# A two-layer decoder step on one core: the first expert pair's rows by a one-hot matmul, four projections ahead of the router, the window-cache copy last

## The reference, cut to what matters

```python
def moe(h, router_w, router_bias, w_gate, w_up, w_down):
    score = sigmoid(h @ router_w)                     # 16 experts
    ... # top-2 experts inside the best of 4 groups; gate = normalised scores
    for e in range(16):
        hid = silu(h @ w_gate[e]) * (h @ w_up[e])     # 1024 -> 512
        out = out + gate[..., e:e + 1] * (hid @ w_down[e])
    return out

def layer_tail(x, mix, p_i, ...):
    h = layer_norm(ALPHA * x + mix, ln1_g, ln1_b)
    h = layer_norm(ALPHA * h + moe(h, ...), ln2_g, ln2_b)
    return h + sigmoid(h @ ple_gate) * (p_i @ ple_proj)
```

## Time and profile before

| | us |
|---|---|
| median of 3 runs | 1172.66 |
| the three runs | 1172.66, 1162.14, 1172.76 |
| the profiled execution | 1171.1 |
| its span, first to last instruction | 1169.3 |
| PE busy in it | 1051.3 (90%) |
| DVE busy | 469.3 (40%) |
| ACT busy | 297.0 (25%) |
| DMA, mean over the span | 297 GB/s |

### The profile page before, as it was taken

How to read it: one execution, slowest core, us unless ns; L and a number is a source line. 1 busy time by engine, 2 the same in 40 slices (tenths; PEclk the granted TensorE clock), 3 DMA queues, 4 the chain that set the end, 5 groups by cost and what they waited for, 6 DMA issues and landing times. The chain is left out here.

```text
span 1169.3 us, 14744 instructions
## 1 busy us (share of the span) xinstructions
PE 1051.3 (90%) x5243; PEld 658.4 (56%) x5243; DVE 469.3 (40%) x1383; ACT 297.0 (25%) x765; POOL 133.3 (11%) x121
## 2 busy tenths in 40 slices
PE   7899998698799999899799989779989999989868
PEld 5688775587554444344477875345755344444347
DVE  2769898932331112011355977472161111111132
ACT  2211798700321111111220015362051011101031
POOL 0000013300001000000004724452000000000000
PEclk9899998799988999999999998889988999999989
DMA  8744696675959999999556975949368899999901
GB/s 287 248 163 149 220 278 215 198 281 198 399 225 408 427 429 428 425 427 428 213 216 235 339 262 178 370 136 382 128 265 370 363 427 426 428 428 426 417 4 38
DMA packets 88943, 347.36 MB, mean 297 GB/s; under 512 B 14690, under 2 KB 52578, under 8 KB 72322
## 3 DMA queue, kind: packets, MB, share of 16 engines
q1 hardware_dynamic: 81186, 313.57, 69.3%
q10 hardware_dynamic: 5376, 24.40, 5.3%
q0 software_dynamic: 2304, 8.39, 1.8%
HBM read 331.66 MB, written 23.04 MB: 303 GB/s over the span
## 5 line engine op out<-in xcount | busy, mean ns | idle before, releaser
L1097 PE MATMUL mh<-expert_ring,x_packed 128*64 128x512 f32 x768 | 173.0, 606 | 14.6 <-DMA expert_ring<-in_moe_w_up 12.7
L1349 DVE TENSOR_TENSOR hid<-mh,silu_gate 128x512 f32<-128x512 f32 x16 | 11.1, 692 | 374.8 <-PE mh L1097 325.9
L1097 PEld LDWEIGHTS mh<-expert_ring,x_packed 128*64 128x64 f32 x768 | 58.2, 140 | 126.3 <-issue 124.3
L1119 PE MATMUL mo<-expert_ring,hid_T 128*64 128x512 f32 x384 | 89.1, 618 | 1.4 <-ACT hid_T L1218 1.4
L495 PE MATMUL ss<-xT,expert_ring 128*128 128x264 f32 x384 | 90.0, 395 | 0.0
L1563 PE MATMUL na<-xT,expert_ring 128*128 128x264 f32 (+1 forms) x336 | 78.8, 398 | 6.1 <-DMA expert_ring<-in_nsa_w_in 3.3
L495 PEld LDWEIGHTS ss<-xT,expert_ring 128*128 128x128 f32 x384 | 73.8, 195 | 13.8 <-issue 0.8
L1563 PEld LDWEIGHTS na<-xT,expert_ring 128*128 128x128 f32 (+1 forms) x336 | 64.6, 193 | 20.2 <-DMA expert_ring<-in_nsa_w_in 4.1
L506 PE MATMUL ss<-xT,expert_ring 128*128 128x264 f32 x256 | 64.1, 406 | 6.1 <-ACT z L385 6.1
L1179 PE MATMUL mg<-acc,expert_ring 128*128 128x264 f32 x256 | 61.7, 406 | 7.2 <-ACT acc L883 7.2
L1097 PE MATMUL mh<-expert_ring_more,x_packed 128*64 128x512 f32 x256 | 58.3, 609 | 7.7 <-DMA expert_ring_more<-in_moe_w_up 3.6
(11 more groups left out here) (377 smaller groups left out, 1541.1 us busy)
## 6 DMA issues: line engine op xcount, KB each, us to landing
expert_ring<-in_moe_w_down SPq DMA_DIRECT2D x24, 2048.0 KB, 22.3
expert_ring<-in_moe_w_gate SPq DMA_DIRECT2D x24, 2048.0 KB, 17.2
expert_ring<-in_moe_w_up SPq DMA_DIRECT2D x24, 2048.0 KB, 23.5
expert_ring<-in_ssd_w_in SPq DMA_DIRECT2D x10, 2048.0 KB, 7.9
expert_ring_more<-in_moe_w_gate SPq DMA_DIRECT2D x8, 2048.0 KB, 14.7
expert_ring_more<-in_moe_w_up SPq DMA_DIRECT2D x8, 2048.0 KB, 19.2
expert_ring_more<-in_moe_w_down SPq DMA_DIRECT2D x8, 2048.0 KB, 22.5
expert_ring<-in_cmp_pages SPq DMA_DIRECT2D x40, 256.0 KB, 4.5
```

The source lines that it names most:

```text
L1097: last = mm(hb[w][s * CAP:(s + 1) * CAP, :], xg[:, k, s * CAP:(s + 1) * CAP], unit(6 * i + 2 * w + s)[:, k * FF:(k + 1) * FF], start=k == ...
L1119: last = mm(ob[2 + a][s * CAP:(s + 1) * CAP, :], ht[:, k, s * CAP:(s + 1) * CAP], unit(6 * i + 4 + s)[:, o:o + 512], start=k == 0, stop=k ...
L1349: V.tensor_tensor(hid[:], hb[1][:], sg[:], ALU.mult).then_inc(hid_ok, 1)
```

## The change

Five edits, four of them in the tail:

1. **Projections 0 to 3** move to right behind PE's part of `ln_a`, into four separate banks. ACT copies their results between the root (L880) and the gain-and-bias steps (L883) of `ln_a`. Projections 4 and 5 stand where 0 and 1 stood, 6 and 7 right behind the rank matmuls.
2. **Pair 0's rows** come from a matmul of `xtok` with `sel1`: 2 x 4 x 3 matmuls of 128 columns. The indirect DMA of pair 0, its `turn_rows` and the slot tokens of pair 0 ahead of it go.
3. **Slot tokens** of all eight pairs are computed inside `gate_up(0)`, one pair's three matmuls ahead of each step k of the up half. `other_slots()` goes; of it the turn of `gover` stays as `gates_over()`.
4. **Unit 7** is loaded right after `wple`, ahead of the wait for the projections. Unit 6 waits as before.
5. **The cache copy** goes from ACT's queue in the Mamba block to SP's queue, behind the last weight load of layer 1.

```diff
@@ Mamba block @@
                     sp.wait_ge(conv_out, 32)
-                    sp.wait_ge(win_out, 16)
...
-                    act.dma_start(O["win_old"], I["cache_win"][:, 1:, :]).then_inc(win_out, 16)
@@ Norm @@
-            def act(self, act):
+            def act(self, act, between=None):
...
                 nc.scalar.activation(self.rs[:, 1, :], self.pv[:, 0:T], ACT.Sqrt, scale=1.0 / D, bias=epst[:, 0:1]).then_inc(s_sqrt, 1)
+                if between is not None:
+                    between()
                 for k in range(KD):
@@ tail, SP @@
+                        load_unit(sp, L, 7, unit(7))
                         sp.wait_ge(e_proj, KD * (L + 1))
-                        for n in range(6, 8):
-                            load_unit(sp, L, n, unit(n))
+                        load_unit(sp, L, 6, unit(6))
...
+                        if L == 1:
+                            sp.dma_start(O["win_old"], I["cache_win"][:, 1:, :]).then_inc(win_out, 16)
@@ tail, PE @@
                         ln_a.pe(pe)
 
+                        def project(m):
+                            if m == 0:
+                                pe.wait_ge(ld_p, 32 * L + 32)
+                            if m >= 4:
+                                pe.wait_ge(e_pre, KD * L + m - 1)
+                            for k in range(2):
+                                last = mm(ob[m if m < 4 else 2 + m % 2][:, 0:T], wple[:, k, m * P:(m + 1) * P], pT[:, k, :], start=k == 0, stop=k == 1)
+                            last.then_inc(e_proj, 1)
+                        for m in range(4):
+                            project(m)
+
                         for k in range(KD):
                             ln_a.out_ready(pe, k)
...
                         for c in range(2, 6):
                             turn_x(c)
-                        project(0)
-                        project(1)
+                        project(4)
+                        project(5)
...
-                        pe.wait_ge(r_gate, 2 * L + 2)
+                        project(6)
+                        project(7)
+
                         pe.wait_ge(r_slots, 4 * L + 2)
-                        pe.wait_ge(r_xtok, 6 * L + 4)
-                        slot_tokens(0, ob[0], 0).then_inc(r_idx, 1)
-                        for m in range(2, KD):
-                            project(m)
-
-                        def other_slots():
-                            pe.wait_ge(r_slots, 4 * L + 4)
-                            for i in range(1, NP2):
-                                last = slot_tokens(i, ob[1], (i - 1) * (1 + NE))
-                            last.then_inc(r_idx, 1)
-                            pe.wait_ge(r_over, L + 1)
+                        pe.wait_ge(r_xtok, 6 * L + 6)
+                        for a in range(2):
+                            for k in range(4):
+                                d = 4 * a + k
+                                for q, (t0, n) in enumerate(tile3):
+                                    last = mm(gb[a][:, k * P:(k + 1) * P], xtok[q][0:n, d * P:(d + 1) * P], sel1[0:n, q, 0:P], start=q == 0, stop=q == 2)
+                            last.then_inc(gathered, 1)
+
+                        def gates_over():
+                            pe.wait_ge(e_pre, KD * (L + 1))
+                            pe.wait_ge(r_over, 2 * L + 1)
...
                                 for k in range(KD):
+                                    if i == 0 and w == 1:
+                                        if k == 0:
+                                            pe.wait_ge(r_gate, 2 * L + 2)
+                                            pe.wait_ge(r_slots, 4 * L + 4)
+                                        slots = slot_tokens(k, ob[1], k * (1 + NE))
+                                        if k == KD - 1:
+                                            slots.then_inc(r_idx, 1)
                                     for s in range(2):
...
-                        turn_rows(0)
                         for i in range(NP2):
                             gate_up(i)
                             if i >= 1:
                                 scatter(i - 1)
                             else:
-                                other_slots()
+                                gates_over()
@@ tail, ACT @@
-                        ln_a.act(act)
+                        def take_projected(m):
+                            act.wait_ge(e_proj, KD * L + m + 1)
+                            A_(ple[:, m, :], ob[m if m < 4 else 2 + m % 2][:, 0:T], ACT.Copy).then_inc(e_pre, 1)
+
+                        def first_projected():
+                            for m in range(4):
+                                take_projected(m)
+                        ln_a.act(act, first_projected)
@@ tail, POOL @@
-                        for i in range(NP2):
+                        for i in range(1, NP2):
@@ tail, DVE @@
-                        dve.wait_ge(r_idx, 2 * L + 1)
-                        slot_gates(0, 1, ob[0])
...
-                                dve.wait_ge(r_idx, 2 * L + 2)
-                                slot_gates(1, NP2 - 1, ob[1])
+                                dve.wait_ge(r_idx, L + 1)
+                                slot_gates(0, NP2, ob[1])
@@ last block @@
                 sp.wait_ge(stored, n_stored[0])
+                sp.wait_ge(win_out, 16)
```

40 lines of the change are left out of this document (17 added, 23 removed).

## The result

| | before | after |
|---|---|---|
| median, us | 1172.71 (1162.14 to 1175.99, 4 runs) | 1187.41 (1183.38 to 1193.97, 4 runs) |
| ratio | | 1.0169, 95% interval 1.0124 to 1.0214 |
| profiled execution, us | 1171.1 | 1187.92 |
| its span, us | 1169.3 | 1186.1 |

The change makes the kernel 1.7% slower. The forecast was 1182 us, 0.8% slower, and it gave the larger chance (0.62) to no change that can be told. The direction of the sum and its largest single term were right; the size was a good half of what was measured, and "slower" had only 0.34.

A forecast was written before the change was run, and what follows sets the result against it. DMA was taken to bound the expert stage, behind a serial chain up to gate_up(0). Layer 0 +12.35, layer 1 -3.9 and the end +1 gave +9.45 us, so 1182 us from the median; range 1166 to 1192.

The forecast's parts named there:

- What bounds the kernel: Expert stage: bound by DMA once its eight buffers are used up, ending a fixed time after units 12 and 13 issue.
- S: Start of gate_up(0) in each layer; forecast to move by +10.35 us in layer 0 and -2.9 in layer 1.
- Projections 0 to 3, layer 0: Ahead of layer 0's router: PE stalls up to 11.5 us for pT and wple; what follows comes 13.25 us later.
- Projections 0 to 3, layer 1: Ahead of layer 1's router: wple lands before PE asks, no stall; sum 0, bounds -0.5 and +1.5 us.
- Pair 0's rows: Ranks to gate_up(0), both layers: 9.5 us instead of 12.36, so -2.9 us per layer, bounds -4.1 and -0.8.
- Slot tokens in the up half: Inside gate_up(0): 7.4 us of slot matmuls delay units 10 and 11; +2.0 us in layer 0, -1.0 in layer 1.
- PE has that slack against DMA.: Behind down(0): turn_rows(1) may wait some 2 us for pair 1's indices, which PE can afford against DMA.
- The cache copy: End of layer 1: copy ends near 1150, 19 us ahead of the end; +1 us for instruction fetch, 0 to 5.
- A: Layer 0: no stall, since the operands land by 309.6; total 1169 us; chance 0.12.
- B: gate_up(0), both layers: slot weight loads hidden under 512-column matmuls, -7.6 us each, total 1167 us; chance 0.08.
- D: Whole kernel: the edits cancel, the stall costing less than 8 us; total 1174 us; chance 0.10.
- C: Stall, gather and slots, both layers: clock stays down longer, some +15, 1197 us; half of it 1189; chance 0.18.

The follow-up runs named there:

- e1_loads: After, with layer 0's weight units 2, 0 and 3 issued behind pT and wple instead of ahead of them: 1171.81 us, ratio to before 1.0032.
- e2_idx: After, with the slot tokens of pairs 1 and 2 computed right behind pair 0's gather, the other six in the up half: ratio to before 1.0102.
- e5_slots_back: After, with all eight pairs' slot tokens moved out of the up half to behind gate_up(0): ratio to before 1.0108.
- e9_no8: After with early operand loads and slot tokens split between the halves and behind down(0), minus the gather's 8-row part: 1155.82 us, one run.
- e11_pairs: After with early operand loads, slot tokens split between the halves and behind down(0), neighbouring gather groups' 8-row parts joined: ratio to before 0.9921.
- e4_late_proj: After, with all eight projections back at their old places: ratio to before 1.0091.
- e3_copy_only: Before, with only the cache copy moved to SP's queue behind layer 1's last weight load: 1170.46 us, ratio to before 1.0011.
- e6_both: After with the edits of e1_loads and e2_idx together: 1165.26 us, ratio to before 0.9977.
- e7_idx_back: e6_both with the other six pairs' slot tokens behind gate_up(0) instead of inside its up half: 1167.27 us, ratio to before 0.9974.

## Why the prediction was right or wrong, step by step

- **What bounds the kernel.** Right in kind: S and the moment at which the transfers become continuous set the end of a layer. But I read that moment off one pair of units, 12 and 13. It held for before, whose units 14 and 15 go 9.3 us later. In after, 12 and 13 went at S + 31.5 and the stage was still 4.5 us longer, because 14 and 15 came 15.8 us behind them. How many bytes had gone by then tells it better: in the 80 us behind S layer 0 moved 418 GB/s before and 344 in after, 5.9 MB less. Units 6 and 7 (4.2 MB) had landed ahead of S in after; the 1.7 MB left are 4 us at 426 GB/s, and up to the last up half the stage is 4.6 us longer.
- **Projections 0 to 3, layer 0.** Right. Wait 11.59 (forecast up to 11.5), ended at 320.8 (320.9), 16 instructions 5.23 us (5.5), L884 at 326.34 (326.8), sigmoid 13.13 later (13.7), ranks 12.64 later (13.25). e1_loads takes it away with the cause named. The Trainium skill's rule on the throttled clock (TensorE: Matmul & The Clock Gate, What's actually happening): the trace agrees, the 16 took 5.23, 5.67 and 6.81 us behind the stall (after, e2_idx, e5_slots_back) and 3.72 without it. None took the 7.0 that I drew from the rule.
- **Projections 0 to 3, layer 1.** Right: no wait, sigmoid 18.35 us behind the norm instead of 18.14.
- **Pair 0's rows.** The term was mis-sized: 10.90 us from ranks to S in layer 0 instead of 9.5, so -1.46 and not -2.9. The projections were as forecast (2.05); the gather took 8.41 us, outside my 5.6 to 8.1, since I priced all 48 instructions by full-height rows, the only ones in the earlier trace rows. e9_no8 and e11_pairs give the reason. The upper end was wrong more grossly: at the lower clock it is 0.310 per instruction, not 0.17. I had scaled a row that was only partly at the lower clock; doubling a clean one gives 0.23, and the changes of height bring the rest.
- **Slot tokens in the up half.** 8.2 us for 7.4; units 10 and 11 at S + 22.2 for 21.35. Nearly right, and the smaller part of the matter. That unit 7 went early shows nowhere: from 350 to 355 the DMA engines had run dry (3 GB/s).
- **"PE has that slack against DMA."** This sentence is the step that failed. I had seen that pair 1's rows might be late by 2 us and dismissed it, because DMA was to be the bound. They were late by 4.29 and 3.16 us: POOL had the indices at S + 23.3 and not at S + 21.6, and in layer 0 the rows took 12.4 us from issue to landing, behind units 10 and 11. PE's gate half of pair 1 is what frees two buffers, so a late PE is a late transfer. The lower clock came with the wait and lengthened that half by 1.8 and 2.5 us more: it takes 8.6 to 9.8 us in all six stretches with the wait (after, e1_loads, e4_late_proj), and 7.09 wherever neither the wait nor slot tokens stand in front of it. The stage cost +4.49 and +1.85 instead of +2.0 and -1.0, 5.3 us in sum. e2_idx and e5_slots_back both undo it. In layer 0 the cost stands clear of the spread (240.2 to 241.0 in after, e1_loads and e4_late_proj, 235.9 in before and e3_copy_only). Layer 1's whole stage does not show it (239.4 to 241.9 against 240.1 and 239.0), but up to the last up half it takes 213.8 to 214.7 us against 211.5 and 210.1; so the sign of my -1.0 was wrong there too.
- **The cache copy.** Right that it is hidden at both places; the +1 for slow instruction fetch was not needed (48.0 us from the second norm to the end, 48.1 before). PE's idle time ahead of the second norm fell, from 3.35 to 1.75 us in layer 0 and from 3.16 to 1.50 in layer 1. The copy has no part in that: e3_copy_only shows 3.32 and 3.21. It is a gain of 1.6 us a layer that I had not forecast, and no run shows which edit brings it. The Trainium skill's rule on engines per DMA (DMA: Bandwidth & Descriptors, How many engines (k)): the trace agrees, 0.51 at the new place too. I had put its end 19 us ahead of the kernel's; it was through by 1170 and the kernel ended at 1186.
- **The rivals.** A, B and D did not happen: the wait was there, and the slots took their full time. C, the clock, came true in part, but in another place than I had it: in pair 1's gate half, behind a wait, and in the last up half. That half of C gives 1189, near the 1187.41 measured, is luck.
- **Left open.** The +1.14 us between the layers is unchanged code, and other executions of it differ by far more. Why the clock falls in one execution and not in another of the same code is open too.

In sum, of the 7.35 us that were missing, 5.3 are the two expert stages, 2.4 the two fronts, 1.1 the stretch between the layers, less 1.1 at the end and 0.4 at the start.

## What to carry to other kernels

When buffers are freed by compute, "the stage is bound by DMA" does not give compute any slack in the pair that frees the next buffers: follow the issue times of several units, not one. Before moving an operation into a gap, ask when its consumer's data are wanted. Here the indices went too late for an indirect DMA that takes 12 us behind two bulk loads; computed between the two halves they cost 1.9 us of PE, and the stage, with the rest put off behind `down(0)`, ends 6.7 and 9.2 us sooner than in after (5.3 and 7.5 of it up to the last up half). A load wanted early belongs ahead of bulk loads in the queue, whatever the queue's throughput: three units behind two small operands were worth 13 us. And compare profiled executions stretch by stretch, with a stretch of unchanged code to tell how much they differ by themselves, and look for stretches that only the clock has lengthened.

## What the runs showed of the hardware

- Small contractions between full ones are dear. Alternating 128-row and 8-row float32 matmuls of 128 columns costs about 0.35 us for each excursion to 8 rows and back, at 0.117 us for a full-height instruction; two neighbouring excursions joined save one. The Trainium skill says of the weight load that its row count doesn't matter (TensorE: Matmul & The Clock Gate, Step-by-step: what each phase is for). For one load the trace agrees (181 ns for 8 rows, 191 for 128), for the mixed stream the measurement decides. That a weight load isn't hidden across such a change is a guess; no run shows it.
- The lower clock came in some executions and not in others of the same code: the gather took 8.41 us in most profiles and 14.9 in those of e6_both and e7_idx_back, both in layer 0; the last pair's up half took 7.09 us or 8.4 to 8.8, in one kernel and from layer to layer.
- An indirect DMA of 128 rows of 4 KB took 12.4 us to land when issued 1 us behind two 2048 KB units, and the next one, issued 1.4 us after it, 17.1 (layer 0 of after). Issued 9 us behind the units, the two took 8.5 us (median, e5_slots_back), and 4.9 us (median, e2_idx) where no unit was on its way.
